# A differential-attention stage whose four small sample groups are taken one by one between the heads of a later stage

## The reference

```
z = rms_norm(x) @ w_in                       # q, k, v of both attentions, rotary on q and k
a = sliding-window attention with sinks      # 8 heads
# differential attention: 4 heads, two score maps c = 0, 1 per head
s = einsum('qhcd,khcd->hcqk', q, k) * scale  # chunk-causal mask for the prompt
p = softmax(s)
o = (p[c=0] - lam * p[c=1]) @ v              # v is 128 wide
d = rms_norm(o, subln_g) * 0.2
h = x + [a ; d] @ w_out
y = rms_norm(h + swiglu(rms_norm(h)))
```

## Time and profile before

| | |
|---|---|
| median of 3 runs | 3065.97 us |
| the profiled execution's own time | 3064.61 us |
| its span, first to last instruction | 3062.8 us |
| TensorE busy over the span | 2747.4 us (90%) |
| VectorE, ScalarE, GpSimd busy | 1555.3, 1156.2, 374.5 us |
| mean granted TensorE clock | 0.942 |
| differential phase, from its first transfer to its last store | 837.8 to 1350 us |

### The profile page before, as it was taken

One profiled execution on the slowest core, in us unless ns is written; L12 is line 12 of the kernel. 1 busy time (PEld: TensorE's weight loads), 2 busy tenths in 40 slices (PEclk: granted clock), 3 DMA queues, 4 the chain that ended last, 5 costly groups with the idle time before them and its releaser, 6 DMA issues. The chain is left out here.

```text
span 3062.8 us, 54590 instructions
## 1 busy us (share of the span) xinstructions
PE 2747.4 (90%) x20536; PEld 1698.7 (55%) x20536; DVE 1555.3 (51%) x2976; ACT 1156.2 (38%) x1995; POOL 374.5 (12%) x465
## 2 busy tenths in 40 slices
PE   0999998377689999958988999999999999999998
PEld 0666665244466677734545565555656556565564
DVE  6555554476679988744542414334142342424326
ACT  2344444466568888853432111211112111121113
POOL 0122221100014555530000000000000000000001
PEclk9999999576669999989998999999999999999999
DMA  4344443111141100122212011010100101011002
GB/s 176 113 164 161 160 164 124 51 47 44 45 81 36 33 9 22 36 76 95 91 49 74 0 41 34 7 41 0 41 12 29 41 0 41 0 41 41 0 14 113
DMA packets 137938, 179.91 MB, mean 59 GB/s; under 512 B 60658, under 2 KB 100562, under 8 KB 136818
## 3 DMA queue, kind: packets, MB, share of 16 engines
q1 hardware_dynamic: 137842, 178.61, 18.0%
HBM read 133.92 MB, written 42.17 MB: 57 GB/s over the span
## 5 line engine op out<-in xcount | busy, mean ns | idle before, releaser
L1984 ACT ACTIVATE silu<-gate_ps,scales 128x352 f32<-128x352 f32 x132 | 73.3, 556 | 1141.2 <-PE up_ps L2024 1141.2
L1915 DVE SCALAR_TENSOR_TENSOR act<-up_ps,scales,silu 128x352 f32<-128x352 f32 x132 | 77.1, 584 | 779.3 <-ACT silu L1984 779.3
L2022 PE MATMUL gate_ps<-ffn_inT_hi,gate_hi 128*128 x1056 | 331.3, 314 | 15.4 <-DVE up_lo L1903 15.4
L1927 DVE SCALAR_TENSOR_TENSOR residual_rows<-down_ps,scales,residual_rows 128x512 f32<-128x512 f32 (+1 forms) x374 | 278.8, 748 | 118.4 <-PE down_ps L2034 117.4
L2024 PE MATMUL gate_ps<-ffn_inT_hi,gate_lo 128*128 x1056 | 331.1, 314 | 0.0
L2023 PE MATMUL gate_ps<-ffn_inT_lo,gate_hi 128*128 x1056 | 331.1, 314 | 0.0
L2024 PE MATMUL up_ps<-ffn_inT_hi,up_lo 128*128 x1056 | 330.0, 313 | 0.0
L2023 PE MATMUL up_ps<-ffn_inT_lo,up_hi 128*128 x1056 | 330.0, 313 | 0.0
L2022 PE MATMUL up_ps<-ffn_inT_hi,up_hi 128*128 x1056 | 330.0, 313 | 0.0
L2032 PE MATMUL down_ps<-down_hi,act_hi 128*128 128x512 f16 (+1 forms) x748 | 283.8, 379 | 0.0
L2033 PE MATMUL down_ps<-down_lo,act_hi 128*128 128x512 f16 (+1 forms) x748 | 283.5, 379 | 0.0
(11 more groups left out here) (271 smaller groups left out, 5651.1 us busy)
## 6 DMA issues: line engine op xcount, KB each, us to landing
w_scan<-in_w_gate SPq DMA_DIRECT2D x16, 704.0 KB, 6.8
w_scan<-in_w_up SPq DMA_DIRECT2D x16, 704.0 KB, 8.1
w_scan<-in_w_down SPq DMA_DIRECT2D x16, 704.0 KB, 4.0
gate<-in_w_gate SPq DMA_DIRECT2D x22, 512.0 KB, 6.0
up<-in_w_up SPq DMA_DIRECT2D x22, 512.0 KB, 7.3
down<-in_w_down SPq DMA_DIRECT2D x22, 512.0 KB, 3.3
keys_values<-in_w_in SPq DMA_DIRECT2D x8, 1152.0 KB, 15.2
x_tile<-in_x SPq DMA_DIRECT2D x17, 512.0 KB, 3.4
```

Source lines behind the costliest of these rows:

```text
L1927: nc.vector.scalar_tensor_tensor(H[0:rows, at:at + 512], YP[(2 * t + n) % 4][0:rows, :], SC[0:rows, S_YI:S_YI + 1], H[0:rows, at:at + 512] ...
L2022: nc.tensor.matmul(out, FH[w][:, k, c], nh, start=k == 0, stop=False)
```

## The change

It does four things.

1. The groups' order is frame block 0, 1, then block 2 with one sample group behind each of its heads, then block 3.
2. The sample's q has a third buffer of its own (`Q1[2]`, `QL[2]`, one tile wide), filled once at the start of the phase, behind everything else. A buffer of `w_out_scan` is dropped, from two to one.
3. The first transfers are the first head's q of frame block 0 alone (4 tiles, 64 KB each); TensorE waits for these before the first group's pieces (`q_first`), and for the other three heads (4 transfers, issued behind the constant rows) before the pieces of the second.
4. The copies of keys are cut in five of 512 KB; the first scores wait for keys 16 to 19, keys 0 to 3 and the constant rows (48 counts in place of 32), each later block for its own copy.

```diff
+SAMPLE = NT // 4
+SAMPLE_BESIDE = 2
...
-        order = [NT // 4] + list(range(NT // 4))
-        self.groups = [Group(4 * s + h, s, n, h) for s, n in enumerate(order) for h in range(HDIF)]
+        order = []
+        for n in range(SAMPLE):
+            for h in range(HDIF):
+                order += [(n, h)] + ([(SAMPLE, h)] if n == SAMPLE_BESIDE else [])
+        self.groups = [Group(i, n, h) for i, (n, h) in enumerate(order)]
+        self.index = {nh: i for i, nh in enumerate(order)}
...
-    def release(self, stage):
-        return 0 if stage < 2 else self.stage_first[stage - 1] + 4
+    def release(self, gr):
+        return 0 if gr.n < 2 or not gr.frame else self.first[self.index[gr.n - 1, 0]] + 4
...
-        QL = [g.sb(f"dq_lo_max{n}", [P, 4, HC, HD + 2], f16, ctx) for n in range(2)]
-        Q1 = [g.sb(f"dqT_hi_hi{n}", [P, HC, 4 * P], f16, ctx) for n in range(2)]
+        QL = [g.sb(f"dq_lo_max{n}", [P, nq, HC, HD + 2], f16, ctx) for n, nq in enumerate((4, 4, 1))]
+        Q1 = [g.sb(f"dqT_hi_hi{n}", [P, HC, nq * P], f16, ctx) for n, nq in enumerate((4, 4, 1))]
...
-                load_q1(0)
+                load_q1(0, slice(0, 2), q_first)
+                copy_keys(0, NT, NKT)
                 load_ql(0)
-                copy_keys(0, NT, NKT)
+                copy_keys(0, 0, 4)
                 sp.wait_ge(mrow_ok, 1)
...
+                load_q1(0, slice(2, HC))
                 load_q1(1)
                 load_ql(1)
-                copy_keys(1, 0, 4)
-                copy_keys(2, 4, NT)
+                for n in range(1, SAMPLE):
+                    copy_keys(n, 4 * n, 4 * n + 4)
+                load_q1(SAMPLE)
+                load_ql(SAMPLE)
...
-                        if stage < 3:
-                            pe.wait_ge(k2_in[stage], 32 if stage == 0 else 16)
+                    if gr.frame and u.k == plan.first[plan.index[gr.n, 0]]:
+                        pe.wait_ge(k2_in[gr.n], 48 if gr.n == 0 else 16)
...
-                pe.wait_ge(q_in[0], q_loads(0))
+                pe.wait_ge(q_first, 16 * groups[0].nq)
```

More of the change, by code:

```diff
@@ L1106, in __init__ @@
         self.first.append(self.K)
-        self.stage_first = [self.first[4 * s] for s in range(len(order))] + [self.K]
         self.pieces = [list(max_pieces(gr)) for gr in self.groups]
@@ L1128, in place_pieces @@
                 end = self.first[g] - 6
-                if end >= k and self.release(self.groups[g].stage) <= end:
+                if end >= k and self.release(self.groups[g]) <= end:
                     slope = max(slope, (cum[g - 1] - done) / (T[end + 1] - T[k]))
@@ L1134, in place_pieces @@
                 must = self.first[p.g.index] - 6 <= k
-                if not must and (done + p.cost / 2 > target or self.release(p.g.stage) > k):
+                if not must and (done + p.cost / 2 > target or self.release(p.g) > k):
                     break
@@ L1199, in phase_differential @@
         CO = g.sb("dconsts", [P, 8], f32, ctx)
-        WB = [g.sb(f"w_out_scan{n}", [P, D], f32, ctx) for n in range(2)]
+        WB = g.sb("w_out_scan", [P, D], f32, ctx)
         MB = [g.ps(f"dmax_ps{n}", [P, 512], f32, ctx) for n in range(2)]
@@ L1212, in phase_differential @@
         stored = [s("stored0"), s("stored1")]
[L1213 to L1216 removed]
+        q_first = s("q1_first_head_in")
+        q_in = [s(f"q1_in{n}") for n in range(3)]
+        ql_in = [s(f"ql_in{n}") for n in range(3)]
+        k2_in = [s(f"k2_in{n}") for n in range(NT // 4)]
+        wo_in = s("w_out_in")
         vt = lambda V, t, h, rows: V[rows, (t * HDIF + h) * VW:(t * HDIF + h + 1) * VW]
         w_out = dram["w_out"].rearrange("a m d -> (a m) d")
[L1219 to L1221 removed]
+        LAST = SAMPLE - 1
+        q_loads = lambda gr: 16 * gr.nq * (gr.n // 2 + 1 if gr.frame else 1)
+        scan_at = {plan.first[plan.index[LAST, m // 2]] + 16 + 8 * (m % 2): m for m in range(KC)}
         ratio_at = {plan.last[gr.index, c] + LAG + 1: (gr, c) for gr in groups for c in range(2)}
```

88 lines of the change are left out of this document (41 added, 47 removed).

## The result

The change makes the kernel slower. Four runs took 3080.51 to 3085.95 us, median 3083.71; the kernel before took 3065.89 (3065.37 to 3068.58) beside them. The ratio is 1.0057, 95% interval 1.0043 to 1.0072: some 17.8 us lost. The profiled execution, the fastest of the four, took 3080.51 us (span 3078.7), 15.9 us over that of before. All but 1.0 of them lie in the differential phase.

What follows compares the result with a forecast made beforehand. TensorE was taken to hold the span nearly everywhere. Terms -20.5 + 20.8 + 0.8 = +1.1 us on the profiled 3064.6 gave 3065.7, and 1.4 for the median gave 3067.1 us, no visible change; 8-in-10 range 3055 to 3078 us.

Steps and rivals of the forecast that it cites:

- Term 1: Start and block 0: first frame scores at 854 instead of 877.05, more pieces beside block 0; -20.5 us, bounds -24 and -17.
- the price of the low part's issue: SyncE's queue at the phase's start: each low part of q takes 0.63 us to issue, four before the constants.
- The wait for the other heads' q: First piece of step 0: four transfers issued right behind the constants cost at most 1 to 2 us more.
- Block 0's other heads: Beside block 0, VectorE paces: five more pieces cost +3.0 us, leftover sample work gone saves 0.5.
- Term 2: Sample groups in block 2: 5.2 us each with VectorE setting the pace, four +20.8 us; bounds 11.2 and 28.
- Term 3: Pieces moved: block 1 +0.6, block 2 +1.1, block 3 -0.9, together +0.8 us.
- What I costed at nothing: Third q buffer's transfers, five copies of keys, single-buffer w_out scan: all in time or with room to spare, no cost.
- B: Block 2: TensorE swallows the sample, VectorE and ScalarE having room over a head; groups cost 11.2, total 3057.5 us; chance 0.25.
- C: Block 2: granted clock falls to 0.50 in sample groups, +3.8 us a group if in each; total 3074.7 us; chance 0.22.
- D: Block 0's start: dense matmuls bring the clock up at once, 3.8 us won; total 3063.3 us; chance 0.13.

Runs made afterwards that it cites:

- both mends: The change with the second head's pieces made ahead of the first unit and maxima, transposes and copy behind sample groups four steps earlier: 3066.73 us, ratio 1.001.
- whole_q_first: The change with all four heads' q of block 0 loaded first and waited for: 3083.36 us, ratio 1.006 to the kernel before.

## Why the prediction was wrong

Forecast: 3067.1 us, no change seen, range to 3078. Measured: 3083.7, slower. The steps that failed are the price of a sample group in block 2 (the largest part), that of the pieces beside block 0, and that of the low part's issue.

**Term 1, the start, right in its mechanism, 1 to 2 us short in size.** The constants release the first scores, at 856.41 where 854 was forecast and 857 was the bound; 0.9 us of that is a later start of the phase. The step that failed is the price of the low part's issue, 0.63 us taken from the single transfer in the earlier trace rows; four in a row cost 1.24 each. Squares after block 0's first head: 883.39 for 881. The wait for the other heads' q that I set at 1 to 2 us does not show among TensorE's waits.

**Block 0's other heads, wrong: +7.1 for +2.5.** The +3.0 for 38 pieces in place of 33 was right on VectorE's work (39.89 to 43.01). I took a busy engine's added work as the whole price. The sample's 28 us at the start had also been time in which 11 pieces for block 0's heads were made. Without them there is no stock. The second and third heads' ends wait in turn: TensorE 2.69 and 2.65 us for maxima, then VectorE 1.93 and 2.05 us for a piece, which is nearly all of the 4.2 us that VectorE idles more. I had put this wait at nothing without a reason. With the second head's pieces made ahead, these heads take 40.5 to 44.5 us in eight traces, against 41.8 before (and 43.6 and 44.0 in the two other traces with the old order): most or all of the 7.1 is gone.

**Term 2, the sample groups, wrong in size and in place.** 5.2 us a group were forecast from engines' sums in eight steps. The runs show 28.9 us for four. A pair without a fall takes 40.2 us, 6.5 over a head alone: 4 x 6.5 = 26.0. The clock's fall in one pair (43.1 for 40.2) adds 2.9. Less the 1.1 us for moved pieces that is 27.8, all but the upper bound that I gave, 28. What I left out is the order: the next head's last piece, maxima, transposes and copy stand among the short steps with the same lead in steps, which is some two thirds of the time. Two more steps of lead took off 5.5 us with no less to do, 2.9 of them the fall. With four, a group costs 5.6, near my 5.2. That is partly luck, since the mechanism under it was VectorE's pace, and 1.9 us less of its load gave only 0.1 to 0.2 us. What makes up the 2.8 us a group over TensorE's own work stays open: ScalarE is the fullest there (11.23 of 12 us), but no run relieves it alone.

**Term 3** went as forecast for block 1 (+0.4 for +0.6). The 0.9 us from four pieces fewer beside block 3 were not seen (0.0). What I costed at nothing (q's third buffer, the copies of keys, the single buffer of the scan) cost nothing: block 3's heads are 45.5, 42.9 and 37.4 us apart, as before.

**The rivals.** B (TensorE swallows it) never came near. C was met in one pair of four in the profile; at 2.9 us a fall it is the smaller part of the miss. I had tied it to the eight steps themselves; none fell with either lead alone, one did with both mends, and whole_q_first had two; what brings a fall about stays open, and kernels that are alike in block 2 had 10.2, 13.7 and 27.3 us of it there. D did not happen: the clock came up at 871.9, 15.5 us after the first frame scores, with dense wide matmuls from the first unit.

The error is 16.6 us by the medians. In the phase's traces it is 13.8: 7.0 from block 2, 4.6 from block 0's other heads, 1.5 from the start and 0.7 from blocks 1 and 3. Another 1.0 lies outside this stretch, 0.9 of it the later start. The last 1.8 is that the change's median lies 3.2 us over its profiled execution, where I had added 1.4.

The range failed at block 0. Term 2 stayed just inside its bound; term 1 came out at -21.5 + 7.1 = -14.4 us, outside its bound of -17, because I had taken no bound for idle time there. With both terms at their upper bounds my sum gives 3077.8 us. The "3061 to 3073" that I called the bounds of terms 1 and 2 is narrower than they are: they give 3054 to 3078.

## What to carry to other kernels

- Before moving small work from a slow stretch into a dense one, measure what it costs by leaving it out: here the kernel without it ended 14.0 us before the old one and 28.9 before the new one. The 28 us that it seemed to take at the start also held the first pieces of what came next.
- A lead counted in steps is a lead in time only while steps are alike. Where short steps are put between long ones, give what is due behind them more steps: two gave most of what there was to gain here, which was 6.6 us of 28.9.
- Sums by engine bound a joint from below. Where three engines are above 80% in it, a move of load from one to the next can cost more than it frees: 2 us off ScalarE and 2 onto VectorE cost 4 a group.
- One trace is one execution. Here the traced ones lay up to 7.5 us off their medians; what held was the stretch that came out alike in nine traces and otherwise in eight.

## What the runs showed of the hardware

- The issue of a transfer in a run of like ones was dearer than of the single one: 1.24 us for 128x8x64 pieces of the low part, 0.58 for the first alone.
- The transfer right behind the constant rows was dear to issue where the rows stood early in the queue: 2.51 us for the single low part, 2.31, 2.43 and 3.05 for a copy of keys, which took 0.74 in the change.
- The constant rows take 9.0 to 10.1 us from issue to use, in the sixteen traces where they end the wait, in fourth or in eleventh place.
- A mean clock is no price. Block 0's other heads took 48.7 us with 15.6 us at 1.2 GHz and 48.8 with 20.5; in block 2 one fall of 10.2 us cost 2.9.
- A subtraction of VectorE on 128 columns that started 0.09 us behind GpSimd's squares took 1.10 us, 0.29 otherwise.
